# Four branch projections as seven block products each instead of eight, in one hybrid decoder step

## What is computed

```
branch outputs -> per-branch D_MODEL projection -> per-channel sigmoid merge gates -> w_out -> residual
```

## Time and profile before

| what | us |
|---|---|
| median of 3 runs | 1034.77 |
| the runs | 1028.83, 1034.77, 1036.46 |
| the profiled execution, its own time | 1034.17 |
| its span | 1032.5 |
| busy: TensorE matmul / weight load / VectorE / ScalarE / GpSimd | 997.0 / 583.4 / 325.3 / 227.5 / 90.7 |

### The profile page before, as it was taken

One profiled execution on the slowest core, in us unless ns is written; L12 is line 12 of the kernel. 1 busy time (PEld: TensorE's weight loads), 2 busy tenths in 40 slices (PEclk: granted clock), 3 DMA queues, 4 the chain that ended last, 5 costly groups with the idle time before them and its releaser, 6 DMA issues. The chain is left out here.

```text
span 1032.5 us, 15099 instructions
## 1 busy us (share of the span) xinstructions
PE 997.0 (97%) x6103; PEld 583.4 (57%) x6103; DVE 325.3 (32%) x812; ACT 227.5 (22%) x486; POOL 90.7 (9%) x131
## 2 busy tenths in 40 slices
PE   7999999999999999999999999999998898998996
PEld 4468776555888898775554444444444343444343
DVE  2124231567666664122431111111111011112164
ACT  2012111367322252001222311111011110110154
POOL 0020040000223220000000000000000000000100
PEclk9999999999999999999999999999999899999998
DMA  9980297120556689545569999999999999999941
GB/s 319 274 251 5 103 201 178 50 82 2 174 174 191 222 288 275 196 155 204 196 250 364 394 425 428 426 426 429 427 430 427 427 427 428 426 426 428 387 131 52
DMA packets 57800, 286.44 MB, mean 277 GB/s; under 512 B 10205, under 2 KB 14534, under 8 KB 45132
## 3 DMA queue, kind: packets, MB, share of 16 engines
q1 hardware_dynamic: 48140, 258.30, 64.7%
q0 software_dynamic: 9360, 27.20, 9.6%
q10 hardware_dynamic: 240, 0.09, 0.1%
HBM read 276.56 MB, written 18.50 MB: 286 GB/s over the span
## 5 line engine op out<-in xcount | busy, mean ns | idle before, releaser
L1227 PE MATMUL ps<-ring,reg_xh 128*64 128x512 f32 x512 | 153.4, 611 | 12.4 <-DMA ring<-in_w_exp_up_dram 8.2
L1227 PE MATMUL ps<-late,reg_xh 128*64 128x512 f32 x336 | 153.1, 610 | 3.6 <-DMA reg_k<-in_w_exp_up_dram 3.6
L1227 PEld LDWEIGHTS ps<-ring,reg_xh 128*64 128x64 f32 x512 | 47.6, 140 | 100.0 <-issue 97.8
L2385 DVE TENSOR_TENSOR reg_xh<-reg_xh,ps 64x512 f32<-64x512 f32 x32 | 22.1, 692 | 253.8 <-ACT reg_xh L1661 253.8
L1661 ACT ACTIVATE reg_xh<-ps 64x512 f32<-64x512 f32 x32 | 34.0, 1062 | 232.6 <-PE ps L1227 232.6
L1202 PEld LDWEIGHTS ps<-reg_xh 128*128 128x128 f32 (+1 forms) x768 | 74.0, 190 | 14.6 <-issue 12.6
L1227 PE MATMUL ps<-reg_k,reg_xh 128*64 128x512 f32 x176 | 80.6, 612 | 0.0
L1202 PE MATMUL ps<-reg_xh 128*128 128x128 f32 (+1 forms) x768 | 78.8, 280 | 0.0
L2639 POOL DMA_INDIRECT y_rows<-reg_xh,slot_row x30 | 29.3, 975 | 545.8 <-ACT reg_xh L1668 525.0
L1227 PEld LDWEIGHTS ps<-late,reg_xh 128*64 128x64 f32 x336 | 45.4, 140 | 50.3 <-issue 49.8
L1668 ACT ACTIVATE reg_xh<-ps 128x512 f32<-128x512 f32 x31 | 18.5, 597 | 150.8 <-PE ps L1255 150.8
(11 more groups left out here) (444 smaller groups left out, 1418.2 us busy)
## 6 DMA issues: line engine op xcount, KB each, us to landing
ring<-in_w_exp_gate_dram SPq DMA_DIRECT2D x21, 2048.0 KB, 25.8
ring<-in_w_in_dram SPq DMA_DIRECT2D x12, 2048.0 KB, 11.0
ring<-in_w_exp_down_dram SPq DMA_DIRECT2D x11, 2048.0 KB, 24.9
ring<-in_w_exp_up_dram SPq DMA_DIRECT2D x11, 2048.0 KB, 31.2
late<-in_w_exp_gate_dram SPq DMA_DIRECT2D x10, 2048.0 KB, 26.1
reg_k<-in_w_exp_up_dram SPq DMA_DIRECT2D x10, 2048.0 KB, 30.7
reg_o<-in_w_exp_down_dram SPq DMA_DIRECT2D x10, 2048.0 KB, 29.6
late<-in_w_exp_up_dram SPq DMA_DIRECT2D x10, 2048.0 KB, 29.2
```

The source lines that it names most:

```text
L1227: last = pe.matmul(out[64 * part:64 * part + 64, :], xb[:, k, :], ws_[part][:, k, :], start=(k == 0), stop=(k == KT - 1))
L2385: dve.tensor_tensor(sg.rearrange("p (m q) -> p m q", m=4), sg.rearrange("p (m q) -> p m q", m=4), ps[64:128, 2 + par, :].rearrange("p (q m ...
```

## The change

The four branch chunks go by the seven-product scheme as well.
- TensorE: `seven_part` issues one matmul of a step, for any input. For the first input, steps 0 and 1 of both chunks come first, then steps 2 to 6 of chunk 0 and of chunk 1; for the second input all seven steps of each chunk in turn. The four chunks take the bank pairs (2, 3), (4, 5), (6, 7) and (0, 1).
- The token sums of the first input go where those of hT were, those of the second over hT itself. For the second input the two token halves change roles in the scheme (`swap`), so that tokens 160 to 319 are the half whose last quarter comes from step 6.
- VectorE: the first chunk's sums come before the mx loop; then token sums, weight sums, and `gate_part` and `gate_last`, which take the place of the loops at L2177 to L2187. ScalarE copies steps 0, 2 and 3, for the second input into three buffers of their own that both chunks use.
- w_out's first tile waits for `normed` at 4 (k = 0) and 7 (k = 4), the tile of the sample tokens for 8.
- The slots of the branch chunks are free at each chunk's step 6 in place of its last output tile.

```diff
@@ -156,7 +156,11 @@
     for n, chunk in enumerate([("gm", c) for c in range(4)] + [("u", c) for c in range(2)]):
         for step in range(7):
             assign([(chunk + (step,), 1)], ((6, 7)[(n + step) % 2],))
-    assign(jobs, range(8))
+    assign(mixing, range(8))
+    for n in range(4):
+        for step in range(7):
+            assign([(("br", n // 2, n % 2, step), 1)], ((2 + 2 * n + step % 2) % 8,))
+    assign(jobs, (2, 3, 4, 5, 6, 7, 0, 1))
     assign(proj, (7, 3, 4, 5, 6, 3))
     plan["expert loop"] = list(read)
...
         pp_flat = pp[:, :, :].rearrange("p t n -> p (t n)")
-        ht1, ht2, ht3, ht4 = (pp_flat[:, 640 * i:640 * i + 640].rearrange("p (k n) -> p k n", k=4) for i in range(4))
-        w_s1 = reg_x[:, 6144:7168].rearrange("p (k n) -> p k n", k=4)
-        w_s2 = [a.rearrange("p (k n) -> p k n", k=2) for a in (reg_x[:, 7168:7680], pp_flat[:, 2560:3072])]
+        def four_sums(flat):
+
+            return [flat[:, 640 * i:640 * i + 640].rearrange("p (k n) -> p k n", k=4) for i in range(4)]
+
+        first_sums, hT_sums = four_sums(pp_flat), four_sums(hT.rearrange("p k n -> p (k n)"))
+        operand = {"gm": (hT, first_sums, 0), "u": (hT, first_sums, 0), "br0": (uT, first_sums, 0), "br1": (obT, hT_sums, 1)}
+        br_kept = [pp_flat[:, 320 * i:320 * i + 320].rearrange("p (m n) -> p m n", m=2) for i in range(3)]
+        s1_s2 = {}
+        for name in ("gm", "u", "br"):
+            flat = [reg_x[:, 6144:7168], reg_x[:, 7168:7680], pp_flat[:, 2560:3072]]
+            if name == "br":
+                flat = [reg_x[:, 2560:3584], reg_kt[:, 0:512], reg_kt[:, 512:1024]]
+            s1_s2[name] = (flat[0].rearrange("p (k n) -> p k n", k=4), [f.rearrange("p (k n) -> p k n", k=2) for f in flat[1:]])
         route = reg_kt
...
+            def seven_part(key, step, i):
+
+                m, k = i // 4, i % 4
+                if i == 0:
+                    begin(key + (step,))
+                    if step in (2, 4, 5):
+                        pe.wait_ge(w_sums, sums_before(key) + {2: 2, 4: 3, 5: 4}[step])
+                x_all, (t1, t2, t3, t4), swap = operand["br%d" % key[1] if key[0] == "br" else key[0]]
+                w, (s1, s2) = quarters(key), s1_s2[key[0]]
+                n1, n2 = tokens_of(swap), tokens_of(1 - swap)
+                near, far = slice(128 * m, 128 * m + 128), slice(256 + 128 * m, 256 + 128 * m + 128)
+                lhs, rhs = {"a11": (w[:, k, near], x_all[:, k, n1]), "a12": (w[:, 4 + k, near], x_all[:, 4 + k, n1]),
+                            "s2": (s2[k // 2][:, k % 2, near], t2[:, k, :]), "s1": (s1[:, k, near], t1[:, k, :]),
+                            "s3": (w[:, k, far], t3[:, k, :]), "s4": (w[:, 4 + k, near], x_all[:, 4 + k, n2]),
+                            "a22": (w[:, 4 + k, far], t4[:, k, :])}[SEVEN[step]]
+                out = ps[:, plan[key + (step,)][0], 160 * m:160 * m + 160]
+                ins = pe.matmul(out, lhs, rhs, start=(i == 0 and step in (0, 1, 3)), stop=(i == 7), skip_group_check=True)
+                if i == 7:
+                    finish(ins, key + (step,))
...
@@ -1099,11 +1136,20 @@
 
             for b in range(NB):
                 evacuated(pe, ("ot", b))
-            for j in range(2):
+            for step in range(2):
                 for c in range(2):
-                    w = chunk_k(("br", j, c))
-                    for m in range(4):
-                        by_channel(("br", j, 4 * c + m), w, m, uT if j == 0 else obT, "mx" if (j, c, m) == (0, 0, 0) else None)
+                    chunk(pe, ("br", 0, c))
+                    for i in range(8):
+                        if i < 4:
+                            evacuated(pe, ("mx", 4 * step + i))
+                        seven_part(("br", 0, c), step, i)
+            pe.wait_ge(br_sums, 4)
+            for c in range(2):
+                steps_of(("br", 0, c), range(2, 7))
+            pe.wait_ge(br_sums, 8)
+            for c in range(2):
+                chunk(pe, ("br", 1, c))
+                steps_of(("br", 1, c), range(7))
             pe.wait_ge(p_in_s, 32)
             for k in range(2):
...
                 for k in ks:
-                    if (c, t) == (0, 0):
-                        pe.wait_ge(normed, k + 1)
+                    if (c, t) == (0, 0) and k in (0, 4):
+                        pe.wait_ge(normed, 4 if k == 0 else 7)
+                    if (c, t, k) == (0, 2, 0):
+                        pe.wait_ge(normed, KT)
...
-            def keep_part(name, c, step, m_half, n_half):
-
-                src = filled(act, (name, c, step))
-                release(act.activation(quarter_of(name, c, m_half, n_half), as_quarter(src), ACT.Copy), (name, c, step))
+            def keep_part(key, step, m_half, n_half, place=None):
+
+                src = filled(act, key + (step,))
+                if place is None:
+                    place = quarter_of(key, m_half, n_half)
+                release(act.activation(place, as_quarter(src), ACT.Copy), key + (step,))
 
             for i in range(18):
...
+
+            for c in range(2):
+                keep_part(("br", 0, c), 0, 0, 0)
+            for c in range(2):
+                keep_part(("br", 0, c), 2, 0, 1)
+                keep_part(("br", 0, c), 3, 1, 1)
+            filled(act, ("br", 0, 1, 6))
+            for c in range(2):
+                for n, step in enumerate((0, 2, 3)):
+                    if c == 1:
+                        act.wait_ge(br_gated, (7, 9, 8)[n])
+                    keep_part(("br", 1, c), step, 0, 0, br_kept[n])
 
             def square_row_sums(t):
...
+            def token_sums(name, signal, before):
+
+                x_all, (t1, t2, t3, t4), swap = operand[name]
+                n1, n2 = tokens_of(swap), tokens_of(1 - swap)
+                dve.tensor_tensor(t1, x_all[:, 0:4, n2], x_all[:, 0:4, n1], ALU.subtract).then_inc(signal, 1)
+                dve.tensor_tensor(t3, x_all[:, 4:8, n2], x_all[:, 0:4, n2], ALU.subtract).then_inc(signal, 1)
+                dve.wait_ge(signal, before + 1)
+                dve.tensor_tensor(t2, x_all[:, 4:8, n2], t1, ALU.subtract).then_inc(signal, 1)
+                dve.wait_ge(signal, before + 3)
+                dve.tensor_tensor(t4, x_all[:, 4:8, n1], t2, ALU.subtract).then_inc(signal, 1)
...
             add_12("u", 1)
+            filled(dve, ("os", NB - 1))
+            dve.wait_ge(v_ready, 3)
+            weight_sums(("br", 0, 0))
...
+            filled(dve, ("u", 1, 6))
+            token_sums("br0", br_sums, 0)
+
+            def gate_part(j, c, step, kept, m_half, n_half):
+
+                key, gate, merged = ("br", j, c), gate_quarter(j, c, m_half, n_half), quarter_of(("br", j, c), m_half, n_half)
+                part = merged if j == 0 else br_kept[(0, 2, 3).index(kept)]
+                src = filled(dve, key + (step,))
+                evacuated(dve, key + (kept,))
+                release(dve.tensor_tensor(part, part, as_quarter(src), ALU.add), key + (step,))
+                evacuated(dve, key + (step,))
+                dve.wait_ge(gm_ready, j + 1)
+                if j == 0:
+                    dve.tensor_tensor(merged, merged, gate, ALU.mult).then_inc(br_gated, 1)
+                    return
+                n = 7 + 3 * c + {1: 0, 4: 1, 5: 2}[step]
+                dve.tensor_tensor(gate, part, gate, ALU.mult).then_inc(br_gated, 1)
+                dve.wait_ge(br_gated, n)
+                dve.tensor_tensor(merged, merged, gate, ALU.add).then_inc(normed, 1)
+
+            def gate_last(j, c, n_half):
+
+                key, gate, merged = ("br", j, c), gate_quarter(j, c, 1, n_half), quarter_of(("br", j, c), 1, n_half)
+                src = filled(dve, key + (6,))
+                release(dve.tensor_tensor(merged if j == 0 else gate, as_quarter(src), gate, ALU.mult), key + (6,))
+                evacuated(dve, key + (6,))
+                if j == 1:
+                    dve.tensor_tensor(merged, merged, gate, ALU.add).then_inc(normed, 1)
+
+            gate_part(0, 0, 1, 0, 0, 0)
+            weight_sums_in_place(("br", 0, 0))
+            gate_part(0, 1, 1, 0, 0, 0)
+            gate_part(0, 0, 4, 3, 1, 1)
+            weight_sums(("br", 0, 1), ("br", 0, 0))
+            gate_part(0, 0, 5, 2, 0, 1)
+            weight_sums_in_place(("br", 0, 1))
+            gate_last(0, 0, 0)
+            for b in range(NB):
+                evacuated(dve, ("ot", b))
+            for i in range(10, 16):
+                evacuated(dve, ("o", i))
+            token_sums("br1", br_sums, 4)
+            gate_part(0, 1, 4, 3, 1, 1)
+            weight_sums(("br", 1, 0), ("br", 0, 1))
+            gate_part(0, 1, 5, 2, 0, 1)
+            gate_last(0, 1, 0)
+            for c in range(2):
+                gate_part(1, c, 1, 0, 0, 1)
+                weight_sums_in_place(("br", 1, c))
+                gate_part(1, c, 4, 3, 1, 0)
+                if c == 0:
+                    weight_sums(("br", 1, 1), ("br", 1, 0))
```

(36 more changed lines are left out.)

79 lines of the change are left out of this document (32 added, 47 removed), and 4 rows, old and new, of the table e.

## The result

| | before | changed |
|---|---|---|
| median, us (8 runs each) | 1033.81 | 1026.53 |
| lowest to highest, us | 1028.83 to 1036.46 | 1023.64 to 1029.12 |
| profiled execution, its span, us | 1034.17, 1032.5 | 1028.65, 1026.6 |

The ratio is 0.9935, with a 95% interval of 0.9911 to 0.9958: 4 to 9 us faster. The forecast was 1026.4 us and a gain of 8.4 us.

A forecast was written before the change was run, and what follows sets the result against it. TensorE was taken to set when the stream of expert weights starts, and the stream when it ends. 1034.77 us with -8.4 for matmuls and 0.0 for waits gave 1026.4 us, range 1020.5 to 1034.0.

The forecast's parts named there:

- The matmuls: Branch stage: 28 steps of 2.172 us, 60.8 in place of 69.25, saving 8.4 us (bounds 8.0 and 9.0).
- The weight loads: Branch stage: 192 more load records, 36.5 us, costed at nothing because matmuls cover them.
- rival 4: Branch stage: weight loads no longer fit under matmuls of 160 columns, 36.5 us more, 1062.9 us; chance 0.02.
- The waits: Branch stage: TensorE never waits for VectorE's sums, cost 0; narrow slacks 0.9, 1.2 and 0.7 us, upper bound 7.5.
- Rival 3: Branch stage: VectorE becomes the bound, two or three narrow slacks fail by 1 to 2 us each, 1030.4; chance 0.06.
- The end of the stage: Between branch stage and w_out: swapping the halves takes the last quarter off the path; cost nothing.
- Pass-through: Before the expert stream: a microsecond saved by TensorE before 529 us is one at the end, so all 8.4 us.
- Rival 1: Expert stage: the weight stream hides the saving, waits grow to 24 us, time 1034.8, or 1030.6 half hidden; chance 0.10.
- Rival 2: From 512 to 529 us: new timing avoids the clock's dip, 3.1 us more gained, 1023.3 us; chance 0.12.
- The sum: Whole kernel: 0.0 for waits, -8.4 for matmuls, 1.7 us around the span kept; median 1026.4 us.
- Rival 5: Branch stage: after a token-sum wait the clock stays at 1.2 GHz, 52 us more, 1078 us; chance 0.04.

The follow-up runs named there:

- no_exchange: The changed kernel with the second input's token halves in the same order as the first's; 1025.48 us, ratio 0.9927.
- half_wout: The changed kernel with half of w_out's k terms left out for the prompt's two token tiles; 1017.51 us, ratio 0.9832.
- q_seven: The changed kernel with q's two chunks by the seven-product scheme as well; 1020.64 us, ratio 0.9854.
- experiments 8 and 9: On another chip, the changed kernel without edits, 1023.64 us (changed_again), and with q by seven products as well, 1020.94 us (q_seven_again).
- late_sums: The changed kernel with four or eight needless VectorE operations ahead of the first input's token sums; 1031.69 and 1035.35 us, one execution each.
- Experiments 3 and 4: The changed kernel with four, then eight needless VectorE operations ahead of the first input's token sums; 1031.69 us (late_sums_4) and 1035.35 us (late_sums_8).
- Experiment 2: The changed kernel with the first input's two chunks one after the other, not side by side (in_turn); 1028.54 us, ratio 0.9969.
- experiment 1: The changed kernel with the second input's token halves in the same order as the first's (no_exchange); 1025.48 us, ratio 0.9927.
- four_more: The changed kernel with step 0 of the last branch chunk computed five times, not once; 1034.63 us, ratio 0.9996.
- in_turn: The changed kernel with the first input's two chunks one after the other, not side by side; 1028.54 us, ratio 0.9969.
- changed_again: The changed kernel without edits, measured again on another chip; 1023.64 us, ratio 0.991.
- q_seven_again: The changed kernel with q by seven products as well, measured again on another chip; 1020.94 us, ratio 0.9877.
- late_sums_4: The changed kernel with four needless VectorE operations ahead of the first input's token sums; 1031.69 us, one execution.
- late_sums_8: The changed kernel with eight needless VectorE operations ahead of the first input's token sums; 1035.35 us, one execution.

## Why the prediction was right

**The matmuls.** 28 steps of 2.172 us make 60.8; the stage took 60.91, to 0.01 us in all six profiles that leave it as it is (changed, no_exchange, half_wout, q_seven, and both of experiments 8 and 9). The pace of u's last four steps was the right row to take; 2.187, the upper bound, would have given 61.2.

**The weight loads.** In the one window of the stage above, the weight load is busy for 60.91 of 60.91 us, beside TensorE busy for the same 60.91. Its 448 loads of 0.190 us would be 85.1 us end to end. So they overlap matmuls and each other. The rule of the Trainium skill's page "TensorE: Matmul & The Clock Gate", in its section on the mechanism of packing small matmuls, that a load overlaps only if it is for another group of rows, does not hold for these 128-row loads, and rival 4 falls with it. The prediction took up only one half of that section: the first paragraph of the same section of the Trainium skill also says that loads into a background weight buffer are pulled ahead of running matmuls. That agrees with these rows, though no run here shows which buffer a load used.

**The waits.** None came, and the slacks were where they were put. VectorE's timeline of the changed kernel:

```profile
402.99 0.49 DVE L2245 TENSOR_TENSOR late<-late,reg_xh 128x320 f32<-128x320 f32 x1
403.51 0.83 DVE L1978 TENSOR_TENSOR pp<-late 128x640 f32<-128x640 f32 x1
...
405.85 0.83 DVE L1983 TENSOR_TENSOR pp<-late,pp 128x640 f32<-128x640 f32 x1
...
414.67 0.49 DVE L2257 TENSOR_TENSOR reg_xh<-reg_xh,ps 128x320 f32<-128x320 f32 x1 [3.81 <-PE ps L975]
415.19 0.49 DVE L2261 TENSOR_TENSOR reg_xh<-reg_xh 128x320 f32<-128x320 f32 x1
415.60 1.22 DVE L2112 TENSOR_TENSOR reg_xh<-ring 128x1024 f32<-128x1024 f32 x1
416.85 0.69 DVE L2114 TENSOR_TENSOR reg_kt<-reg_xh,ring 128x512 f32<-128x512 f32 x1
417.46 0.68 DVE L2115 TENSOR_TENSOR reg_kt<-reg_xh,ring 128x512 f32<-128x512 f32 x1
```

The mx loop's last product (L2245) ends at 402.99 + 0.49 = 403.48 and is asked for at 399.19 + 2 x 2.172 + 3 x 0.27 = 404.34: 0.9 us, predicted 0.9. The token sums end at 405.85 + 0.83 = 406.68 and are asked for at 407.94: 1.26 us, predicted 1.2. Chunk 1's weight sums end at 418.14 and its step 2 begins at 418.81: 0.67 us, predicted 0.7. The third (L2112 to L2115) starts after VectorE sat idle 3.81 us for TensorE, so this slack is set by how soon step 4 ends and not by how much VectorE has to do before it. In the late_sums kernels TensorE's steps moved back together with VectorE's sums, and it stayed. Experiments 3 and 4 also confirm the size of the first: four operations more pushed the sums back by 3.4 us (4 operations of 0.86 us) and made a wait of 2.3, so some 1.1 to 1.2 us of slack were there. Rival 3 is out. Experiment 2 shows what the slack rests on: the order.

**The end of the stage.** Here a reason failed, at no cost to the sum. "Swapping the halves takes the last quarter off the path" takes for granted that it was on it; experiment 1 shows it was not, with 5 us between its end and its first reader.

**Pass-through.** One for one, as argued from the idle DMA of the earlier trace rows. Waits for expert weights are 16.0 us as before, four_more gives back the whole gain for 8.69 us of work, half_wout shows no limit by the stream for an arrival another 10.6 us sooner, and the expert loop keeps its length in all of them. Rival 1, with 24 us of waits, is out; a share of a microsecond or two would hide in the spread.

**The clock.** Rival 2 named a real thing, and it stays open whether the change moves it. From the stage's end to the first expert matmul the same work took 63.36 us before and 61.69 in the changed kernel, because the dip of the clock in it was shorter. All ten profiles in which this work is whole show one of three lengths: 60.0 (no_exchange, in_turn), 61.7 (changed, changed_again, q_seven_again) and 63.4 us (before, both late_sums, four_more, q_seven). The four profiles that leave the stage latest, from 462.98 us on, all have 63.4, but q_seven, which leaves it at 454.01, has it too, and each is one execution. Over all executions there is no gain of the size of rival 2's 3.1 us, which would be 0.003 of the mean granted clock: it was 0.9860 in the nine of no_exchange beside 0.9875 before, and 0.9872 in the six of changed_again beside 0.9857 before. The dip between 60 and 100 us comes and goes in one and the same kernel, and with the tail it is part of why the profiled execution lies above the median. That the changed kernel gave 1023.64 us on the second occasion and not 1026.5 is left open; with ratios of 0.991 and 0.9935 and their intervals it need not have a cause.

**The sum.** One term was taken over as it was, without a reason: the 1.7 us around the span, which are 2.0 to 2.1 now. The stage's 8.3 less these 0.4 is 8.0 us; the comparisons with the kernel before gave 6.7, 7.5 (no_exchange) and 9.3 us (changed_again), each with 2 to 3 us to either side.

**Rival 5's price was wrong.** It had the clock stay at 1.2 GHz for the rest of the stage, 52 us. The runs put it at under 2 us on top of the wait. With that, a slack missed by 2.3 us would have ended near 1026.4 + 2.3 + 1.7 = 1030.4 us, still faster than before: late_sums_4, with just this wait, took 1031.69. Only its combination with a wait of 5 us and more reaches the time of before, as late_sums_8 did (1035.35).

## What to carry to other kernels

Where the seven-product scheme already runs in one stage, its step time there times the number of steps gives the next stage's time to 0.2% (60.8 for 60.91 us here, 30.4 for 30.48 in q), provided that the sums fit in the time of the steps that need none. Put the steps that read no sums first, of two chunks if one has too few: here that is worth 3.2 of 8.3 us. Before moving work off a path, look for the first instruction that reads it: the last quarter without the exchange was read 5 us after it was ready.

## What the runs showed of the hardware

- A wait of TensorE of only 2.3 us in a stretch that is otherwise busy throughout was followed by a granted clock of 0.57 over its next step, most of it at 1.2 GHz (3.91 us in place of 2.17). A wait of 5.7 us cost hardly more (4.08), and in both the step behind it was at full speed. A wait of 1.8 us in in_turn left the clock at 1.00.
- Executions of one kernel differ in where the clock falls: the same 170 matmul records took 15.02 us at 0.77 in one profile of the changed kernel and 11.90 at 1.00 in the other (changed_again). Two profiles of the changed kernel reach the branch stage at 399.19 and 394.25 us and differ by 5.4 us in span, while the stage takes 60.91 in both; compare lengths of stages, not starts.
- 448 weight loads of 0.190 us fitted into 60.91 us of matmuls without a gap, though they add up to 85.1 us.
